# Two places per slot, in place of three, where a projection stream is interrupted, and VectorE and ScalarE steps placed anew

## The chip, the cores and the metric

One core of one Trainium2 chip runs the whole layer. The metric is the device time in microseconds (us) of one execution, as the median of three runs. TensorE is PE in the profile, VectorE DVE, ScalarE ACT, GpSimd POOL, SyncE SP.

## The reference

```python
h = x * (1.0 + scale[:, None, :]) + shift[:, None, :]          # adaLN from c
proj = h @ w_in + b_in                                         # 1024 tokens, 6664 columns
# branch A, 8 heads of 64, per block of 128 queries
z = einsum('bhtd,bhsd->bhts', qb, kb) * scale
log_rem = where(causal, log_sigmoid(-z), 0.0)
suffix = cumsum(log_rem, reverse=True) - log_rem
attn = where(causal, exp(log_sigmoid(z) + suffix), 0.0)        # times v
y_sb = (heads * silu(sb_z)) @ w_sb_proj
# branch B, 4 heads of 128, a gated recurrence computed by chunks
mq, mk = split(silu(causal_depthwise_conv(concat(ml_q, ml_k), conv_w, conv_b)))
hm = head_norm(mlstm_chunkwise(mq, mk, ml_v, i_pre, log_f), ml_norm_g)
y_ml = (hm * sigmoid(ml_o) * silu(ml_z)) @ w_ml_proj
y = (sigmoid(g_sb) * y_sb + sigmoid(g_ml) * y_ml) @ w_out
out = layer_norm(2 ** 0.25 * x + (1 + gate) * y, ln_g, ln_b)
```

## The kernel before

A prologue builds h, transposed, as a high and a low part (hH, hL; the weights likewise, wH, wL), so that each fp32 product is three fp32r matmuls. Then comes a loop of four iterations i = 0 to 3, then the remaining gate projections, the merge of the branches and the output with its norm. The change touches the loop.

One iteration computes one pair of attention heads (branch A), one mLSTM head (branch B), and the projections of the next. The projections are a stream of 432 matmuls of 128x512 (`project(i, lo, hi)`, L617): nine jobs of 48, numbered 0 to 431, each job in two halves that fill proj_ps[0] and [1]. All other PE work interrupts this stream. After the first 48 come twelve slots s = 0 to 11, then a tail of 45. A slot is a block of 128 queries against up to 512 keys; `n_keys(s)` is 128, 256, 384, 512, 128, 512, 256, 512, 384, 512, 512, 512.

What a slot s does, in order of its data: PE makes the scores of both heads h into z_ps[0] and [1] (`scores`, L701 to L703). ACT takes exp into ez (`odds`, L973). DVE caps and masks it (`cap_odds`, L1462, L1465). ACT takes ln(1 + e), then exp of its negative, into rem (`remainders`, L982, L986). DVE scans rem backwards (`stick_left`, L1478, one scan per head). POOL multiplies ez by it (L556): these are the attention weights. In the next slot PE transposes them, 128x128 at a time (`turn_weights`, L716), into at_ps, which is bank 7 for both heads, and ACT copies them to SBUF (`turned`, L994). Then PE multiplies them by v (`weighted_values`, L732).

Because at_ps is one bank, head 1's transposes wait until ACT has copied head 0's out (semaphore at_out), and they are made at different places in the stream:

```python
scores(i, s)
project(i, a, b)
if s > 0:
    turn_weights(i, s - 1, 0)
mlstm_first(i, s)
project(i, b, c_)
if s > 0:
    turn_weights(i, s - 1, 1)
mlstm_second(i, s)
mlstm_third(i, s)
project(i, c_, d)
if s > 0:
    weighted_values(i, s - 1)
```

Branch B uses misc_ps[0] and [1]. `conv_sum(i, k)` on DVE, k = 0 to 3, computes the two halves of the convolution of k (k = 0, 1) and of q (k = 2, 3); `conv_exps`, `conv_bound`, `conv_sigmoid` and `conv_silu` turn it into m_k (index 0) and m_q (index 1). `chunk_weights` and `mask_chunk_weights` make the chunk weights m_w. `mlstm_third` transposes m_k in slot 2 and m_v in slot 3. In slots 4 to 11 a chunk cc = s - 4 goes through PE (`mlstm_first`, L745 to L752), DVE (`chunk_scores`, L1567, L1569), PE (`mlstm_second`, L759) and DVE (`chunk_values`, L1579 to L1587). The first needs m_q, and both misc banks drained by the step that used them last.

Each engine runs its own list in order, so a wait holds up all that stands behind it. The place of an ACT or DVE step among projections is set by `events`: a number of stream position for each evacuation, weight split and gate step (o_log, z_log, z_exp, z_mul); `tasks(i, lo, hi)` issues those of a stretch. Steps of other kinds hang on the slots through `place0`, `place1` and `place2`, which stand behind the first, the second and again the second stretch of a slot.

## Time and profile before

| what | value |
|---|---|
| three runs | 1025.34, 1029.36, 1030.14 us, median 1029.36 us |
| the profiled execution | 1025.17 us, of which its span 1023.4 us |
| PE busy | 953.4 us, 93% of the span |
| DVE busy | 602.2 us, 59% |
| ACT busy | 457.2 us, 45% |
| POOL busy | 173.0 us, 17% |
| mean granted TensorE clock | 0.981 of full speed |

The span runs from the first to the last instruction of one profiled execution. Busy time is the sum of an engine's instructions; matmuls overlap, so PE at 93% does not say how near it is to its peak. In the loop, the transposes of L716 run from 136.0 to 681.1 us of the span.

### The profile page before, as it was taken

Reading aid. Unit: us, or ns where it says so; the run is one execution under the profiler, and the core shown is the slowest. Engines: PE = TensorE matmul, PEld = TensorE weight load, DVE = VectorE, ACT = ScalarE, POOL = GpSimd, SP = SyncE. Lnnn points to the kernel's source line nnn. Section 1 sums busy time; section 2 is a strip of 40 time slices with the busy share of each in tenths; the row PEclk is TensorE's granted clock in tenths of the full one; section 3 lists DMA queues with packets and bytes.
Section 4 is the critical chain, followed back from the end, with each engine's and each line's share of the span. In section 5 each row is a group of like instructions: output and inputs, shape, how many; then the busy total and the mean of one; then the engine's idle time right before and its main releaser. Section 6 shows DMA issues by size and latency. Waiting matters only on the chain.

```text
span 1023.4 us, 14224 instructions
## 1 busy us (share of the span) xinstructions
PE 953.4 (93%) x4965; PEld 754.4 (74%) x4965; DVE 602.2 (59%) x1100; ACT 457.2 (45%) x811; POOL 173.0 (17%) x145
## 2 busy tenths in 40 slices
PE   2399999899999899998999998999999999988995
PEld 1367877677877688776788776788778888866883
DVE  2854786564875566865657856553653333264766
ACT  1133456554475463665554765434743222251221
POOL 1101021322032231122420132311100000001220
PEclk9689999999999999999999999999999999999998
DMA  8702121011311102211113111115712111233232
GB/s 287 250 11 67 43 63 42 22 34 29 93 40 41 31 20 61 72 40 31 30 31 93 42 31 33 31 50 165 242 58 73 50 42 41 93 105 101 83 105 100
DMA packets 78083, 73.64 MB, mean 72 GB/s; under 512 B 4792, under 2 KB 66360, under 8 KB 78044
## 3 DMA queue, kind: packets, MB, share of 16 engines
q1 hardware_dynamic: 73116, 58.31, 19.8%
q0 software_dynamic: 2624, 8.54, 2.5%
q10 hardware_dynamic: 2304, 6.29, 1.6%
q8 instruction: 23, 0.38, 0.2%
q14 instruction: 16, 0.13, 0.0%
HBM read 64.59 MB, written 8.40 MB: 71 GB/s over the span
## 4 chain that ended last, share of the span: by engine, by line
PE 86%; DVE 4%; ACT 4%; issue 3%; DMA 2%; SPq 1%; POOL 0%; ACTq 0%; DVEq 0%; POOLq 0%
PE bank L617 45%; PE bank L597 9%; PE bank L599 9%; PE bank L598 9%; PE bank L732 3%; PE bank L716 3%; PE bank L701 2%; PE bank L686 1%; DMA x_rows<-in_x 1%; ACT rem L982 1%; DMA a_raw<-in_w_ada 1%; PE bank L703 1%; PE bank L702 1%; DVE a_acc L1302 1%; PE bank L759 1%
## 5 line engine op out<-in xcount | busy, mean ns | idle before, releaser
L617 PE MATMUL bank<-hH,wH 128*128 128x512 f32 x704 | 288.7, 410 | 0.6 <-DVE wL L1316 0.6
L617 PE MATMUL bank<-hH,wL 128*128 128x512 f32 x704 | 276.7, 393 | 0.0
L617 PE MATMUL bank<-hL,wH 128*128 128x512 f32 x704 | 275.5, 391 | 0.0
L556 POOL TENSOR_TENSOR ez<-ez,rem 128x512 f32<-128x512 f32 (+3 forms) x96 | 135.0, 1425 | 423.4 <-DVE rem L1478 423.4
L1316 DVE SCALAR_TENSOR_TENSOR wL<-w_raw,wH 128x512 fp32r<-128x512 f32 (+1 forms) x122 | 94.0, 772 | 142.3 <-ACT wH L901 141.2
L617 PEld LDWEIGHTS bank<-hH,wH 128*128 128x128 f32 x704 | 132.5, 188 | 35.7 <-issue 10.6
L617 PEld LDWEIGHTS bank<-hH,wL 128*128 128x128 f32 x704 | 132.2, 188 | 29.3
L617 PEld LDWEIGHTS bank<-hL,wH 128*128 128x128 f32 x704 | 132.7, 189 | 24.6 <-issue 1.0
L901 ACT ACTIVATE wH<-w_raw 128x512 fp32r<-128x512 f32 (+1 forms) x122 | 75.5, 621 | 103.1 <-PE bank L599 76.2
L1478 DVE TENSOR_TENSOR_SCAN rem<-rem,ones 128x512 f32<-128x512 f32 (+3 forms) x96 | 88.5, 964 | 28.5 <-ACT rem L986 28.5
L994 ACT ACTIVATE at<-bank 128x512 f32<-128x512 f32 (+3 forms) x96 | 46.2, 481 | 42.3 <-PE bank L716 42.3
L973 ACT ACTIVATE ez<-bank 128x512 f32<-128x512 f32 (+3 forms) x96 | 41.8, 488 | 50.0 <-PE bank L703 49.5
L716 PE MATMUL bank<-ident,ez 128*128 128x128 f32 x288 | 47.9, 275 | 13.9 <-ACT at L994 13.9
L1462 DVE TENSOR_SCALAR ez<-ez 128x512 f32<-128x512 f32 (+3 forms) x80 | 27.5, 344 | 53.5 <-ACT ez L973 52.5
L716 PEld LDWEIGHTS bank<-ident,ez 128*128 128x128 f32 x288 | 35.7, 139 | 29.8 <-ACT at L994 20.4
L597 PE MATMUL bank<-hH,wH 128*128 128x512 f32 (+1 forms) x144 | 57.4, 399 | 0.0
L598 PE MATMUL bank<-hL,wH 128*128 128x512 f32 (+1 forms) x144 | 57.4, 399 | 0.0
L586 POOL TENSOR_TENSOR yL<-yT,yH 128x1024 fp32r<-128x1024 f32 x6 | 17.2, 2861 | 236.2 <-ACT yH L1243 236.2
L599 PE MATMUL bank<-hH,wL 128*128 128x512 f32 (+1 forms) x144 | 57.1, 396 | 0.0
L597 PE MATMUL bank<-hH,yH 128*128 128x512 f32 x128 | 51.9, 406 | 5.4 <-POOL yL L586 3.0
L599 PE MATMUL bank<-hH,yL 128*128 128x512 f32 x128 | 52.1, 407 | 0.0
L598 PE MATMUL bank<-hL,yH 128*128 128x512 f32 x128 | 52.0, 407 | 0.0
(234 smaller groups left out, 1466.1 us busy)
## 6 DMA issues: line engine op xcount, KB each, us to landing
w_raw<-in_w_in SPq DMA_DIRECT2D x104, 256.0 KB, 2.9
a_raw<-in_w_ada SPq DMA_DIRECT2D x16, 512.0 KB, 4.6
x_rows<-in_x SPq DMA_DIRECT2D x8, 512.0 KB, 7.7
raw<-in_w_ada POOLq DMA_DIRECT2D x8, 512.0 KB, 5.9
x_in<-in_x SPq DMA_DIRECT2D x8, 512.0 KB, 4.0
out_y<-res SPq DMA_DIRECT2D x8, 512.0 KB, 2.9
raw<-in_w_out SPq DMA_DIRECT2D x10, 256.0 KB, 4.3
m_w<-bm_scratch ACTq DMA_DIRECT2D x4, 512.0 KB, 4.0
```

Source lines behind the costliest of these rows:

```text
L556: g.tensor_tensor(e, e, r, ALU.mult).then_inc(a_done[h], 1)
L597: t.matmul(ps, aH, bH, start=k == 0, stop=False)
L598: t.matmul(ps, aH, bL, start=False, stop=False)
L599: return t.matmul(ps, aL, bH, start=False, stop=k == kt - 1)
L617: ins = t.matmul(proj_ps[half][:], w, a, start=(r == 0), stop=(r == JOB_MM // 2 - 1))
L716: ins = t.transpose(at_ps[:, b * P:(b + 1) * P], ez[s % 2][h][:, b * P:(b + 1) * P], ident[:])
L732: ins = t.matmul(y_ps[64 * h:64 * h + 64, tt], v_tok[:, j, 64 * h:64 * h + 64], at_sb[h][:, b * P:(b + 1) * P], start=b == 0 and not conti ...
L901: a.activation(wH[:, slot, :, 0:width], w_raw[:, slot, :, 0:width], ACT.Copy, scale=scale)\
L973: a.activation(ez[s % 2][h][:, 0:w], z_ps[h][:, 0:w], ACT.Exp).then_inc(ex_done[h], 1)
L994: a.activation(at_sb[h][:, 0:w], at_ps[:, 0:w], ACT.Copy).then_inc(at_out[h], 1)
L1316: v.scalar_tensor_tensor(out=wL[:, slot, :, 0:width], in0=w_raw[:, slot, :, 0:width], scalar=scale, in1=wH[:, slot, :, 0:width], op0=ALU.m ...
L1478: v.tensor_tensor_scan(back, back, ones[:, 0:1].to_broadcast((P, w)), first, ALU.mult, ALU.min)\
```

## The change

It does these things:

- `turn_weights` handles both heads in one go and writes into z_ps[0] and [1], from which ACT has taken the exp of this slot's scores by then; bank 7 is not used for it. `scores` of the next slot waits in its turn until ACT has copied the transposed weights out.
- A slot has two interruptions. The first is `mlstm_first`, `weighted_values(s - 2)` and `scores`; the second is both heads' `turn_weights(s - 1)`, `mlstm_second` and `mlstm_third`. Stretches are 8, 8, 16 matmuls in slots 0 to 2, and 7, 6, 14 after (the first two run through on PE); the tail has two stretches in place of three.
- The transposes of next_v move from stream position 24 into slot 0, with ACT's copy.
- On DVE, `chunk_scores` moves ahead of `cap_odds`, and `chunk_values` right behind `stick_left`. `chunk_weights` moves from slot 0 to slot 1, and the mask from slot 1 to slot 2, behind the scans. `conv_bound(1)` stands ahead of the scans of slot 3, `conv_silu(1)` right behind them.
- On ACT, `turned` of both heads stands behind the second stretch's tasks; `conv_exps(1)` and `conv_sigmoid(1)` come earlier in slot 3; the exp of the chunk weights stands behind `conv_sigmoid(0)`.
- The gate steps have separate places for DVE's and ACT's halves (o_cap, z_cap, z_sum are DVE's).

```diff
@@ line 127 @@
...
     at, out = PRE, []
     for s in range(NS):
-        sizes = (10, 10, 12) if s < 3 else (9, 9, 9)
+        sizes = (8, 8, 16) if s < 3 else (7, 6, 14)
         row = [at]
...
@@ line 141 @@
...
     at = segments()[0][-1][-1]
-    third = (JOB_MM * NJ - at) // 3
-    return [at, at + third, at + 2 * third, JOB_MM * NJ]
+    return [at, at + (JOB_MM * NJ - at) // 2, JOB_MM * NJ]
...
@@ line 150 @@
     n = NJ
-    found = [(JOB_MM * 4 + 6, 2, "o_log", 0, 0), (JOB_MM * 5 + 6, 2, "z_log", 0, 0),
-             (JOB_MM * 5 + 14, 2, "z_exp", 0, 0), (JOB_MM * 5 + 22, 2, "z_mul", 0, 0)]
+    found = [(JOB_MM * 4 + 4, 2, "o_cap", 0, 0), (JOB_MM * 4 + 15, 2, "o_log", 0, 0),
+             (JOB_MM * 5 + 4, 2, "z_cap", 0, 0), (JOB_MM * 5 + 20, 2, "z_log", 0, 0),
+             (JOB_MM * 5 + 32, 2, "z_sum", 0, 0), (JOB_MM * 6 + 1, 2, "z_exp", 0, 0),
+             (JOB_MM * 6 + 12, 2, "z_mul", 0, 0)]
     for j in range(n):
...
@@ line 209 @@
...
         proj_ps, z_ps, y_ps, misc_ps = bank[0:2], bank[2:4], bank[4], bank[5:8]
-        at_ps = bank[7]
...
@@ line 693 @@
...
                     r = slice(64 * h, 64 * h + 64)
-                    if s > 0:
+                    if s > 1:
+                        pe.wait_ge(at_out[h], i * NS + s - 1)
+                    elif s > 0:
                         pe.wait_ge(ex_done[h], i * NS + s)
...
@@ line 702 @@
...
-            def turn_weights(i, s, h):
-                if h == 0:
-                    if s > 0:
-                        pe.wait_ge(at_out[1], i * NS + s)
-                    else:
-                        pe.wait_ge(dec_drained, 1)
-                else:
-                    pe.wait_ge(at_out[0], i * NS + s + 1)
-                pe.wait_ge(a_done[h], i * NS + s + 1)
-                for b in range(n_keys(s) // P):
-                    ins = t.transpose(at_ps[:, b * P:(b + 1) * P], ez[s % 2][h][:, b * P:(b + 1) * P], ident[:])
-                ins.then_inc(at_filled[h], 1)
+            def turn_weights(i, s):
+                for h in range(2):
+                    if s + 1 < NS:
+                        pe.wait_ge(ex_done[h], i * NS + s + 2)
+                    pe.wait_ge(a_done[h], i * NS + s + 1)
+                    for b in range(n_keys(s) // P):
+                        ins = t.transpose(z_ps[h][:, b * P:(b + 1) * P], ez[s % 2][h][:, b * P:(b + 1) * P], ident[:])
+                    ins.then_inc(at_filled[h], 1)
...
@@ line 760 @@
...
             def mlstm_third(i, s):
+                if s == 0:
+                    for n in range(2):
+                        pe.wait_ge(m_drained[n], m_count(n, i, F_V))
+                        if n == 0:
+                            pe.wait_ge(drained[1], job(i, -2) + 1)
+                        transposes(n, [next_v[:, cc * P:(cc + 1) * P] for cc in range(4 * n, 4 * n + 4)])
                 if s == 2:
...
@@ line 775 @@
...
                 segs, _ = segments()
-                project(i, 0, 24)
-                for n in range(2):
-                    pe.wait_ge(m_drained[n], m_count(n, i, F_V))
-                    if n == 0:
-                        pe.wait_ge(drained[1], job(i, -2) + 1)
-                    transposes(n, [next_v[:, cc * P:(cc + 1) * P] for cc in range(4 * n, 4 * n + 4)])
-                project(i, 24, PRE)
+                project(i, 0, PRE)
                 for s in range(NS):
-                    a, b, c_, d = segs[s]
+                    start, _, middle, end = segs[s]
+                    mlstm_first(i, s)
+                    if s > 1:
+                        weighted_values(i, s - 2)
                     scores(i, s)
-                    project(i, a, b)
+                    project(i, start, middle)
                     if s > 0:
-                        turn_weights(i, s - 1, 0)
-                    mlstm_first(i, s)
-                    project(i, b, c_)
-                    if s > 0:
-                        turn_weights(i, s - 1, 1)
+                        turn_weights(i, s - 1)
                     mlstm_second(i, s)
                     mlstm_third(i, s)
-                    project(i, c_, d)
-                    if s > 0:
-                        weighted_values(i, s - 1)
+                    project(i, middle, end)
+                weighted_values(i, NS - 2)
                 ends = tail()
                 project(i, ends[0], ends[1])
-                turn_weights(i, NS - 1, 0)
+                turn_weights(i, NS - 1)
                 project(i, ends[1], ends[2])
-                turn_weights(i, NS - 1, 1)
-                project(i, ends[2], ends[3])
                 weighted_values(i, NS - 1)
...
@@ line 991 @@
...
                     act.wait_ge(pv_done[h], i * NS + s)
-                a.activation(at_sb[h][:, 0:w], at_ps[:, 0:w], ACT.Copy).then_inc(at_out[h], 1)
+                a.activation(at_sb[h][:, 0:w], z_ps[h][:, 0:w], ACT.Copy).then_inc(at_out[h], 1)
...
@@ line 1034 @@
...
                         continue
-                    if what == "z_mul":
+                    if what in ("o_cap", "z_cap", "z_sum", "z_mul"):
                         continue
...
@@ line 1095 @@
...
             def place0(i, s):
-                if s == 5:
+                if s == 6:
                     store_y(i, 0)
...
@@ line 1108 @@
...
                     load_forget_row(i)
-                if s == 1:
-                    act.wait_ge(w_sum, i + 1)
-                    a.activation(m_w[:], m_w[:], ACT.Exp).then_inc(w_exp, 1)
-                if s == 3:
-                    conv_exps(i, 1)
+                    token_major(i, F_V, v_tok)
...
                     conv_sigmoid(i, 0)
+                    act.wait_ge(w_sum, i + 1)
+                    a.activation(m_w[:], m_w[:], ACT.Exp).then_inc(w_exp, 1)
                 if s == 3:
                     token_major(i, F_MV, m_vtok)
-                    conv_sigmoid(i, 1)
...
                 tasks(i, -1, 24, last)
-                token_major(i, F_V, v_tok)
                 act.wait_ge(sig_log, i * 2 + 1)
...
                     odds(i, s)
+                    if s == 3:
+                        conv_exps(i, 1)
                     tasks(i, p0, p1, last)
...
                     remainders(i, s)
+                    if s == 3:
+                        conv_sigmoid(i, 1)
+                    tasks(i, p1, p2, last)
                     if s > 0:
                         turned(i, s - 1, 0)
-                    tasks(i, p1, p2, last)
+                        turned(i, s - 1, 1)
                     place1(i, s)
-                    if s > 0:
-                        turned(i, s - 1, 1)
                     place2(i, s)
...
                 turned(i, NS - 1, 0)
-                tasks(i, ends[1], ends[2], last)
                 turned(i, NS - 1, 1)
...
                 a.activation(small[:, 24:32], small[:, 24:32], ACT.Exp, scale=-0.5).then_inc(rstd_exp, 1)
-                tasks(i, ends[2], ends[3], last)
+                tasks(i, ends[1], ends[2], last)
                 store_y(i, 1)
...
@@ line 1489 @@
...
                         continue
-                    if what == "o_log":
+                    if what == "o_cap":
                         for h in range(2):
...
                         v.tensor_scalar(m_gate[:], m_gate[:], EXP_CAP, None, ALU.min).then_inc(o_capped, 1)
-                    elif what == "z_log":
+                    elif what == "z_cap":
                         cap_sig(i * 2 + 1)
-                    elif what == "z_exp":
+                    elif what == "z_sum":
                         dve.wait_ge(sig_log, i * 2 + 2)
...
@@ line 1623 @@
...
             def place0(i, s):
-                if s == 5:
-                    gate_y(i, 0)
                 if s >= 4:
...
@@ line 1633 @@
...
                     conv_bound(i, 0)
-                if s >= 4:
-                    chunk_values(i, s - 4)
...
                     pair_gate(i)
+                if s == 1:
                     chunk_weights(i)
-                if s == 1:
-                    mask_chunk_weights(i)
                     conv_sum(i, 2)
                 if s == 2:
+                    conv_sum(i, 3)
                     weighted_keys(i)
-                    conv_sum(i, 3)
-                if s == 3:
-                    conv_bound(i, 1)
-                    conv_silu(i, 1)
...
@@ line 1660 @@
...
                     p0, p1, p2, p3 = segs[s]
+                    place0(i, s)
                     cap_odds(i, s)
...
                         conv_silu(i, 0)
-                    place0(i, s)
+                    if s == 3:
+                        conv_bound(i, 1)
+                    if s == 5:
+                        gate_y(i, 0)
                     tasks(i, p0, p1, last)
                     stick_left(i, s)
+                    if s == 2:
+                        mask_chunk_weights(i)
+                    if s == 3:
+                        conv_silu(i, 1)
+                    if s >= 4:
+                        chunk_values(i, s - 4)
                     tasks(i, p1, p2, last)
...
```

PE in slot 6, between stretches of L617 (before) and L618 (changed); the rows left out are projections, score terms and further blocks. Before:

```order
L716 MATMUL bank<-ident,ez 128x128 [waits a_done0,at_out1]
L716 MATMUL bank<-ident,ez 128x128
...
L745 MATMUL bank<-m_q,m_k 128x128 [waits misc_drained0]
L750 MATMUL bank<-m_vtok,m_ktok 128x129 [waits misc_drained1]
L752 MATMUL bank<-m_state,m_q 128x129
...
L716 MATMUL bank<-ident,ez 128x128 [waits a_done1,at_out0]
L716 MATMUL bank<-ident,ez 128x128
...
L759 MATMUL bank<-m_vtok,m_s 128x129 [waits misc_drained0]
...
L732 MATMUL bank<-at,v_tok 64x128 [waits at_out0]
L732 MATMUL bank<-at,v_tok 64x128 [waits at_out1]
```

In the changed kernel:

```order
L744 MATMUL bank<-m_q,m_k 128x128 [waits misc_drained0]
L749 MATMUL bank<-m_vtok,m_ktok 128x129 [waits misc_drained1]
L751 MATMUL bank<-m_state,m_q 128x129
L731 MATMUL bank<-at,v_tok 64x128 [waits at_out0]
L731 MATMUL bank<-at,v_tok 64x128 [waits at_out1]
...
L704 MATMUL bank<-kH,qH 128x512 [waits at_out0]
...
L704 MATMUL bank<-kH,qH 128x512 [waits at_out1]
...
L715 MATMUL bank<-ident,ez 128x128 [waits a_done0,ex_done0]
L715 MATMUL bank<-ident,ez 128x128
L715 MATMUL bank<-ident,ez 128x128 [waits a_done1,ex_done1]
L715 MATMUL bank<-ident,ez 128x128
...
L758 MATMUL bank<-m_vtok,m_s 128x129 [waits misc_drained0]
```

The two heads' transposes stand together and wait for the exps (ex_done), the scores wait for the copies (at_out), and mlstm_first stands at the slot's head.

ACT in slot 7 (L973 and L968 exp of scores, L982 to L986 and L977 to L981 remainders, L994 and L989 copies of the turned weights, L1035 the gate's exp, L1026 its ln). Before:

```order
L973 ACTIVATE ez<-bank 128x512 [waits at_filled0,z_done0]
L973 ACTIVATE ez<-bank 128x512 [waits at_filled1,z_done1]
L1035 ACTIVATE sig<-sig 128x1024 [waits z_sum]
...
L982 ACTIVATE rem<-ez 128x512 [waits a_done0,ez_capped0]
L982 ACTIVATE rem<-ez 128x512 [waits a_done1,ez_capped1]
L986 ACTIVATE rem<-rem 128x512 [waits ln_done0]
L986 ACTIVATE rem<-rem 128x512 [waits ln_done1]
L994 ACTIVATE at<-bank 128x256 [waits pv_done0,at_filled0]
...
L923 ACTIVATE next_q<-bank,h_col 128x512 [waits proj_filled0]
L994 ACTIVATE at<-bank 128x256 [waits pv_done1,at_filled1]
```

In the changed kernel:

```order
L968 ACTIVATE ez<-bank 128x512 [waits at_filled0,z_done0]
L968 ACTIVATE ez<-bank 128x512 [waits at_filled1,z_done1]
...
L977 ACTIVATE rem<-ez 128x512 [waits a_done0,ez_capped0]
L977 ACTIVATE rem<-ez 128x512 [waits a_done1,ez_capped1]
L981 ACTIVATE rem<-rem 128x512 [waits ln_done0]
L981 ACTIVATE rem<-rem 128x512 [waits ln_done1]
L1026 ACTIVATE sig<-sig 128x1024 [waits sig_capped]
...
L918 ACTIVATE next_q<-bank,h_col 128x512 [waits proj_filled0]
L989 ACTIVATE at<-bank 128x256 [waits pv_done0,at_filled0]
L989 ACTIVATE at<-bank 128x256 [waits pv_done1,at_filled1]
```

The gate step between the exps and the remainders, which waits for a sum on DVE, has gone to slot 8; another, whose input is capped in the slot before, stands behind the remainders.

DVE from the last step of m_k in slot 2 on (L1541 and L1534 conv_silu(0), L1478 and L1471 scans, L1316 and L1309 weight splits, L1560 and L1553 weighted keys, L1527 to L1531 and L1520 to L1524 conv_sum(3)). Before:

```order
L1541 SCALAR_TENSOR_TENSOR m_k<-m_num,m_k 128x1024 [waits conv_sig]
L1478 SCALAR_TENSOR_TENSOR rem<-rem,ones 128x384 [waits rem_done0]
L1478 SCALAR_TENSOR_TENSOR rem<-rem,ones 128x384 [waits rem_done1]
...
L1316 SCALAR_TENSOR_TENSOR wL<-w_raw,wH 128x512 [waits wH_done]
...
L1560 TENSOR_TENSOR m_ktok<-bank,h_tok 128x512 [waits misc_filled0]
...
L1560 TENSOR_TENSOR m_ktok<-bank,h_tok 128x512 [waits misc_filled1]
L1527 TENSOR_SCALAR m_q<-conv_in,h_col 128x512 [waits proj_drained1]
...
L1531 SCALAR_TENSOR_TENSOR m_q<-conv_in,h_col,m_q 128x512 [waits dve_step]
...
L1316 SCALAR_TENSOR_TENSOR wL<-w_raw,wH 128x512 [waits wH_done]
```

In the changed kernel:

```order
L1534 SCALAR_TENSOR_TENSOR m_k<-m_num,m_k 128x1024 [waits conv_sig]
L1471 SCALAR_TENSOR_TENSOR rem<-rem,ones 128x384 [waits rem_done0]
L1471 SCALAR_TENSOR_TENSOR rem<-rem,ones 128x384 [waits rem_done1]
L1546 TENSOR_TENSOR m_w<-m_w,notbefore 128x1024 [waits w_exp]
L1520 TENSOR_SCALAR m_q<-conv_in,h_col 128x512 [waits proj_drained1]
...
L1524 SCALAR_TENSOR_TENSOR m_q<-conv_in,h_col,m_q 128x512 [waits dve_step]
...
L1553 TENSOR_TENSOR m_ktok<-bank,h_tok 128x512 [waits misc_filled0]
...
L1553 TENSOR_TENSOR m_ktok<-bank,h_tok 128x512 [waits misc_filled1]
...
L1309 SCALAR_TENSOR_TENSOR wL<-w_raw,wH 128x512 [waits wH_done]
...
L1309 SCALAR_TENSOR_TENSOR wL<-w_raw,wH 128x512 [waits wH_done]
```

The mask of the chunk weights (L1546) now follows the scans of slot 2, and conv_sum(3) stands ahead of the weighted keys, which no longer have a split ahead of them.

## Rows read from the trace of the kernel before

**Rows 1.** The page: shares of the chain that ended last, by engine.

```profile
PE 86%; DVE 4%; ACT 4%; issue 3%; DMA 2%; SPq 1%; POOL 0%; ACTq 0%; DVEq 0%; POOLq 0%
```

**Rows 2.** Waits of PE: us in total, times, longest.

```profile
PE bank L716 <- ACT at L994: 13.9, 12, 2.9
```

**Rows 3.** Timeline of PE: start us, us, operation, idle before; iteration 2, slot 7.

```profile
486.76 0.44 PE L716 MATMUL bank<-ident,ez 128*128 128x128 f32 x2 [2.94 <-ACT at L994]
```

**Rows 4.** Timelines of ACT, then DVE, same slot.

```profile
483.30 1.06 ACT L1035 ACTIVATE sig<-sig 128x1024 f32<-128x1024 f32 x1 [3.60 <-DVE sig L1501]
...
482.05 1.22 DVE L1501 TENSOR_TENSOR sig<-sig,m_gate 128x1024 f32<-128x1024 f32 x1
```

**Rows 5.** Timeline of PE, iteration 2, around slot 4.

```profile
447.70 0.39 PE L617 MATMUL bank<-hH,wL 128*128 128x512 f32 x1
448.02 0.88 PE L732 MATMUL bank<-at,v_tok 128*64 128x128 f32 x12
...
449.32 0.50 PE L617 MATMUL bank<-hH,wH 128*128 128x512 f32 x1
...
453.03 0.40 PE L617 MATMUL bank<-hH,wL 128*128 128x512 f32 x1
...
454.42 0.39 PE L617 MATMUL bank<-hH,wL 128*128 128x512 f32 x1
...
455.54 0.39 PE L617 MATMUL bank<-hL,wH 128*128 128x512 f32 x1
```

**Rows 6.** Timeline of DVE, iteration 2, slots 1 to 2.

```profile
420.15 1.23 DVE L1548 TENSOR_TENSOR m_w<-m_w,h_tok 128x1024 f32<-128x1024 f32 x1
...
426.06 0.69 DVE L1316 SCALAR_TENSOR_TENSOR wL<-w_raw,wH 128x512 fp32r<-128x512 f32 x1 [1.21 <-ACT wH L901]
...
427.27 1.22 DVE L1553 TENSOR_TENSOR m_w<-m_w,notbefore 128x1024 f32<-128x1024 f32 x1
428.40 0.54 DVE L1527 TENSOR_SCALAR m_q<-conv_in,h_col 128x512 f32<-128x512 f32 x1
...
431.22 0.29 DVE L1462 TENSOR_SCALAR ez<-ez 128x256 f32<-128x256 f32 x1
...
432.03 1.22 DVE L1541 SCALAR_TENSOR_TENSOR m_k<-m_num,m_k 128x1024 f32<-128x1024 f32 x1
433.69 1.81 DVE L1478 TENSOR_TENSOR_SCAN rem<-rem,ones 128x384 f32<-128x384 f32 x2 [0.44 <-ACT rem L986]
435.44 1.41 DVE L1316 SCALAR_TENSOR_TENSOR wL<-w_raw,wH 128x512 fp32r<-128x512 f32 x1
436.78 1.28 DVE L1560 TENSOR_TENSOR m_ktok<-bank,h_tok 128x512 f32<-128x512 f32 x2
```

**Rows 7.** Timeline of PE, iteration 2: m_k transposes, then mlstm_first of slot 4.

```profile
434.74 1.04 PE L686 MATMUL bank<-ident,m_k 128*128 128x128 f32 x8
...
451.90 0.39 PE L745 MATMUL bank<-m_q,m_k 128*128 128x128 f32 x2
```

**Rows 8.** Groups of DVE by form, loop: same operation behind and clear of scans.

```profile
L1536 DVE TENSOR_SCALAR sig<-sig 128x1024 f32<-128x1024 f32 x4 | 6.9, 1728 | 0.0
...
L1536 DVE TENSOR_SCALAR m_num<-m_num 128x1024 f32<-128x1024 f32 x4 | 2.7, 685 | 0.0
```

**Rows 9.** Timelines of ACT, then DVE, iteration 2, slot 3.

```profile
441.98 1.15 ACT L982 ACTIVATE rem<-ez 128x512 f32<-128x512 f32 x2 [0.85 <-DVE ez L1465]
...
443.69 2.34 DVE L1478 TENSOR_TENSOR_SCAN rem<-rem,ones 128x512 f32<-128x512 f32 x2 [1.27 <-ACT rem L986]
445.94 1.73 DVE L1536 TENSOR_SCALAR sig<-sig 128x1024 f32<-128x1024 f32 x1
```

**Rows 10.** Timelines of PE, then DVE, iteration 2, slot 9.

```profile
500.40 0.51 PE L701 MATMUL bank<-kH,qH 64*128 64x512 f32 x2
...
505.27 2.46 DVE L1478 TENSOR_TENSOR_SCAN rem<-rem,ones 128x512 f32<-128x512 f32 x2 [0.24 <-ACT rem L986]
...
509.29 0.34 DVE L1579 TENSOR_SCALAR m_tmp<-bank,h_tok 128x129 f32<-128x129 f32 x1
```

## The prediction

> **What bounds the kernel now.** I read the page first: PE holds 86% of the chain that ended last [rows 1]. A change to the loop can gain in two ways only: less PE work, or less time in which PE waits. The view of waits gives the second: PE waits for ACT's copy of the turned weights (at, L994) 13.9 us in all, 12 times, so 3 per iteration and 3.5 us of each [rows 2]. It is the one wait of PE inside the loop that is worth an edit. The longest of the three lies in slot 7: 2.94 us before head 1's transposes [rows 3]. Its cause is on ACT and DVE: the gate's exp (L1035) stands ahead of the remainders and waits 3.60 us for a sum (L1501) that DVE starts only at 482.05; everything behind it on ACT, the copy of head 0 too, is late by that much [rows 4].
>
> **The change, term by term.** Times are for one iteration, then times four.
>
> *A. The waits of at.* Head 1's transposes no longer share a bank with head 0's, and the gate's exp no longer stands ahead of the remainders. ACT's copies are now due only at the next slot's `weighted_values`, some 4 us later (14 projections of 0.23 us, and `mlstm_first`). The pitch 0.23 is 1.39 us over six starts, 453.03 to 454.42 [rows 5]. All of 13.9 us goes: -13.9.
>
> *B. One interruption fewer per slot.* From 454.42 to 455.54 is 1.12 us for two projections (0.46) and a block of four transposes and mlstm_second (six instructions, 0.44 of it the transposes) [rows 5]; that is the work itself, and what a block of 128-column transposes costs beyond it I cannot tell from zero. Entering `weighted_values` does cost: 0.32 us after the last projection, at 447.70 to 448.02, where the pitch is 0.23 [rows 5]; that entry stays, behind `mlstm_first`. So B is 0, with bounds of -0.1 and +0.1 per slot (both from this entry), which I take at 0 since full-width blocks enter free. The transposes of next_v move with the same work: 0.
>
> *C. The transposes of m_k in slot 2 need `conv_silu(0)`.* Before, DVE was done with it at 433.2 (432.03 and 1.2) and PE asked at 434.74: 1.5 us in hand [rows 6, 7]. In the changed kernel `chunk_weights` stands where the mask stood, 1.87 us (1.26 from 420.15 on, and a second step of 0.6) for 1.13 (427.27 to 428.40) [rows 6], so DVE is 0.74 us later; and PE comes after 32 projections of the two slots where it came after 36, so 0.9 us earlier. That leaves -0.1: a wait of about 0.2 us, +0.8 in four iterations (bounds 0 and +2).
>
> *D. `mlstm_first` of slot 4 needs `conv_silu(1)` and stands at the slot's head.* This is the largest term against. PE, from the transposes of m_k to that point: 17.2 us before (434.74 to 451.90) [rows 7]; five projections fewer (1.1), no `weighted_values` and no scores of slot 4 (together 1.5: 447.70 to 449.32 less one pitch, and 0.1 at the exit), one block of four transposes fewer (0.4), and a short wait of 0.1 gone [rows 5]: 14.0 us. DVE, from the end of `conv_silu(0)`, which is the same moment: scans of 384, 1.75 (433.69 to 435.44); the mask, 1.13; `conv_sum(3)`, 2.8 as `conv_sum(2)` (428.40 to 431.22); weighted keys, 1.2 (the 1.28 of the pair, less the overlap with the next); two splits, 1.25 (0.69 each, as at 426.06, less the overlap); the cap of head 0 in two steps, 0.5 (a little over the 0.4 of slot 2's, 431.22 on) [rows 6]. That is 8.6. From there ACT's logarithms and exps take 1.75 until the scans start (441.98 to 443.69, and the handover), the scans 2.25 (443.69 to 445.94) [rows 9], `conv_silu(1)` 1.2: 13.8. So far no wait. But one row says that what follows scans is held up. The same operation, 1024 elements, took 1728 ns right behind the scans of slot 3 and 685 ns elsewhere [rows 8], and the split right behind the scans of slot 2 took 1.41 us where clear of scans it takes 0.69 (435.44 and 426.06) [rows 6]. POOL's product of head 0 runs at those times. In the changed kernel the mask stands behind the scans of slot 2 and `conv_silu(1)` behind those of slot 3: +0.7 and +1.0, and some 0.2 for the second product inside `conv_sum(3)`. DVE is then done at 15.8, 1.8 us after PE asks. Bounds: 0.4 without any of it (the sigmoid on ACT and the copy of the last m_v bank come then last) and 2.3 with another full hold. I take 1.8, since both rows lie where the steps will stand: +7.2 (bounds +1.6 and +9.2).
>
> The Trainium skill (SBUF — State Buffer, "Who interferes with whom") has a rule for this: VectorE with two SBUF inputs, or in a two-port mode, and GpSimd lock each other out for a whole instruction. By that rule the three two-input steps of `conv_sum(3)` are candidates too, and D would be nearer 2.3 than 1.8.
>
> *E. The other slot heads.* `mlstm_first` of slots 5 to 11 needs `chunk_values` of the slot before. The tightest is slot 9 of 512 keys with an evacuation ahead: before, from the start of its scores (500.40) to the end of the scans 7.25 us (505.27 and 2.38), and 0.65 for the two steps that drain the banks, each as the 0.34 of m_tmp: 7.9 [rows 10]. PE comes back after scores 0.9, 13 projections 3.0, six transposes 0.7, mlstm_second 0.2 and 14 projections 3.2, with 0.1 for the exit of the block: 8.1. In hand: 0.2 us; in the other 512-key slots, which have no evacuation there or start later on PE, about 0.7 (the 0.6 of an evacuation more). So E is 0 (upper bound 0.3 per iteration, +1.2). Weight splits, gate steps and stores stay hidden: DVE and ACT are idle before the next exps, and if that cover were gone each would cost its own 0.6 to 1.2 us. SP's loads and POOL's products keep their order.
>
> **Sum.** -13.9 + 0.8 + 7.2 + 0 = -5.9 us. Against the profiled execution of 1025.2 us that is 1019.3. That execution and the three runs lie 5 us apart (1025.2 to 1030.1) with a mean of 1027.5, so for a median I forecast **1021.5 us**, 0.8% under the median shown of 1029.36 and 0.6% under that mean.
>
> **Rivals.**
> 1. *All is covered.* The holds don't occur (POOL's product happens to run later), D is 0.4 and C is 0. -13.9 + 1.6 = -12.3: 1015. For it: the sum without holds is 13.8 against 14.0. Against it: both rows of holds. Chance 0.17.
> 2. *The hold spreads.* Each two-input step of DVE behind a scan is held by the product of POOL. D is 2.3, C 0.5, E 0.3, so 3.1 per iteration: -13.9 + 12.4 = -1.5, 1026. For it: 1.04 and 0.72 us in the rows where it could be seen [rows 6, 8]. Against it: most steps behind scans in slots 4 to 11 read PSUM, and slot 9 shows none. The page's rule cited above is this rival's. Chance 0.28.
> 3. *Slower: the slot heads become the bound.* PE now stands still at every `mlstm_first` until DVE has drained the banks of the slot before; before, it came to that point after scores and nine projections, 3 us later. If the chain exp, cap, ln, exp, scan, values is later by L than I have it, slot 9 costs L - 0.2 and three more slots L - 0.7 each. It decides from L = 1.3: 1.1 + 1.8 = 2.9 per iteration, 11.6 in all, a net of +5.7. At L = 1.5 it is 1.3 + 2.4 = 3.7, so +8.9: 1036. For it: a chain of seven handovers with 0.2 us in hand. Against it: the chain's length is measured [rows 10]. Chance 0.13.
> My own case has 0.42.
>
> **Chances and range.** About 0.5%, 5 us, is what a measurement of this kernel can tell from no change. Faster by more: rival 1 (0.17), four fifths of my case (0.34), a little of rival 2: 0.52. Within: a fifth of my case (0.08), and 0.23 of rival 2: 0.31. Slower: rival 3 (0.13) and the rest of rival 2: 0.17. The range runs from 1013, rival 1 with B's gain, to 1032, rival 2 with the upper bounds of C and E and the scatter of the runs. My own case alone is 1017 to 1026.
>
> **What would show each step.** A: the wait of PE's transposes for ACT (at) falls from 13.9 us to under 1. D: in slot 4, PE idle before `mlstm_first` for 1 to 2.3 us, released by DVE's m_q or by the copies of m_v; DVE's `conv_silu(1)` over 2 us long instead of 1.2. C: a wait of some tenths before the transposes of m_k. The mask in slot 2 about 1.9 us long. E: in slots 5 to 11 no wait above 0.3 us. B: the pitch from block to block unchanged. Wrong would be: waits at most slot heads (rival 3), no wait in slot 4 (rival 1), or a wait on scores for the copies, which I have at none since ACT is done 3 us ahead.

## The result, and the profile after

The changed kernel takes **1021.68 us** (median of 11 runs, 1017.64 to 1022.96), the kernel before, run beside it on the same chip, 1027.53 us (11 runs, 1024.6 to 1030.76). The ratio is 0.9934 with a 95% interval of 0.9919 to 0.995: 0.66% faster (the two medians lie 5.85 us, 0.57%, apart). The profiled execution of the changed kernel took 1021.37 us with a span of 1019.6 us and a mean granted clock of 0.975; that of before 1025.17, 1023.4 and 0.981.

The page of the changed kernel: the engines, the clock by slices, and the chain by engine.

```profile
PE 955.2 (94%) x4965; PEld 765.9 (75%) x4965; DVE 600.2 (59%) x1100; ACT 456.5 (45%) x811; POOL 177.3 (17%) x145
...
PEclk9689998999999999999999999999999999999998
...
PE 82%; DVE 10%; issue 2%; ACT 2%; DMA 2%; SPq 1%; POOL 0%; DVEq 0%; ACTq 0%; POOLq 0%
```

DVE's part of the chain went from 4% to 10% and ACT's from 4% to 2% [rows 1]: what PE waits for has changed hands. The view of PE's waits between 120 and 700 us, where the four iterations lie, has one row where it had another one before [rows 2]:

```profile
PE bank L744 <- DVE m_q L1534: 8.4, 4, 2.1
```

So the wait for `at` is gone altogether, and in its place stands one wait per iteration, of the first chunk matmul of slot 4 (`mlstm_first`) for `conv_silu(1)`. PE's timeline of iteration 2 there (columns as in [rows 3]):

```profile
448.20 0.48 PE L744 MATMUL bank<-m_q,m_k 128*128 128x128 f32 x2 [2.12 <-DVE m_q L1534]
...
450.22 0.42 PE L705 MATMUL bank<-kL,qH 64*128 64x128 f32 x2
...
451.81 0.63 PE L618 MATMUL bank<-hH,wL 128*128 128x512 f32 x1
452.24 0.63 PE L618 MATMUL bank<-hH,wH 128*128 128x512 f32 x1
...
454.04 0.39 PE L618 MATMUL bank<-hH,wH 128*128 128x512 f32 x1
454.27 0.40 PE L618 MATMUL bank<-hL,wH 128*128 128x512 f32 x1
```

The wait is the one forecast. What follows it was not: the projections start 0.43 us apart at 452, where at 454 they are back at 0.23. The view by windows says why (columns: window, its length, busy time of PE, PEld, DVE, ACT and POOL, granted clock, DMA share, GB/s), behind the waits of iterations 0 and 2:

```profile
164.00:166.00 2.00, 2.00 (x19) 1.55 (x15) 0.06 (x1) 0.00 (x0) 0.00 (x0) 0.50 0.00 0
166.00:168.00 2.00, 2.00 (x5) 1.61 (x6) 1.10 (x4) 1.35 (x6) 0.10 (x1) 0.50 0.00 0
168.00:170.00 2.00, 2.00 (x6) 1.55 (x6) 0.13 (x1) 0.00 (x0) 0.80 (x2) 0.54 0.00 0
...
450.00:452.00 2.00, 2.00 (x11) 1.69 (x10) 0.50 (x2) 0.92 (x5) 0.00 (x0) 0.50 0.00 0
452.00:454.00 2.00, 2.00 (x8) 1.57 (x7) 0.74 (x2) 0.44 (x3) 0.91 (x2) 0.72 0.00 0
```

The granted clock is at the lower of its two levels (0.5, that is 1.2 GHz) for some 6.8 us in iteration 0 and 3.4 us in iteration 2, and at 1.00 everywhere else in the iterations. The trace of before has no such stretch in its iterations.

What the stretches cost can be read from the lengths of the iterations, taken from the scores of slot 0 to the next scores of slot 0. In the changed kernel:

```profile
123.53 0.34 PE L704 MATMUL bank<-kH,qH 64*128 64x128 f32 x2
...
267.93 0.34 PE L704 MATMUL bank<-kH,qH 64*128 64x128 f32 x2
...
409.25 0.34 PE L704 MATMUL bank<-kH,qH 64*128 64x128 f32 x2
...
552.09 0.34 PE L704 MATMUL bank<-kH,qH 64*128 64x128 f32 x2
```

and before:

```profile
268.72 0.34 PE L701 MATMUL bank<-kH,qH 64*128 64x128 f32 x2
...
412.15 0.34 PE L701 MATMUL bank<-kH,qH 64*128 64x128 f32 x2
```

Before, an iteration lasts 143.4 us. After, iterations 0, 1 and 2 last 144.40, 141.32 and 142.84. Iteration 1, which has no stretch, is 2.1 us shorter than before; beside it the stretch of 6.8 us cost 3.1 and the one of 3.4 us cost 1.5. Four iterations without a stretch would save 8.4 us; less the 4.6 of the two stretches this is 3.8, the difference of the two spans.

DVE in iteration 2, slots 2 to 4, where the terms C and D stand:

```profile
430.62 1.22 DVE L1534 SCALAR_TENSOR_TENSOR m_k<-m_num,m_k 128x1024 f32<-128x1024 f32 x1
431.75 1.80 DVE L1471 TENSOR_TENSOR_SCAN rem<-rem,ones 128x384 f32<-128x384 f32 x2
433.47 1.98 DVE L1546 TENSOR_TENSOR m_w<-m_w,notbefore 128x1024 f32<-128x1024 f32 x1
435.37 1.24 DVE L1520 TENSOR_SCALAR m_q<-conv_in,h_col 128x512 f32<-128x512 f32 x1
...
443.58 2.34 DVE L1471 TENSOR_TENSOR_SCAN rem<-rem,ones 128x512 f32<-128x512 f32 x2 [0.67 <-ACT rem L981]
446.14 1.93 DVE L1534 SCALAR_TENSOR_TENSOR m_q<-sig,m_q 128x1024 f32<-128x1024 f32 x1 [0.22 <-ACT sig L1084]
```

The mask takes 1.98 us where it took 1.22, the first step of `conv_sum(3)` 1.24 where it took 0.54, and `conv_silu(1)` 1.93 where `conv_silu(0)` takes 1.22 [rows 6]. POOL's products lie beside them:

```profile
432.78 3.55 POOL L557 TENSOR_TENSOR ez<-ez,rem 128x384 f32<-128x384 f32 x2 [8.72 <-DVE rem L1471]
444.89 4.31 POOL L557 TENSOR_TENSOR ez<-ez,rem 128x512 f32<-128x512 f32 x2 [8.56 <-DVE rem L1471]
```

### The profile page after: what moved, and what is told of

Its sections match the earlier page's. It is cut to its first block, busy times and chain, and to the rows that moved or that the text cites. A ratio compares the mean times of both kernels' runs of the same rounds, so it can differ in the third digit from the quotient of the medians.

```text
span 1019.6 us, 14219 instructions
## 1 busy us (share of the span) xinstructions
PE 955.2 (94%) x4965; PEld 765.9 (75%) x4965; DVE 600.2 (59%) x1100; ACT 456.5 (45%) x811; POOL 177.3 (17%) x145
## 4 chain that ended last, share of the span: by engine, by line
PE 82%; DVE 10%; issue 2%; ACT 2%; DMA 2%; SPq 1%; POOL 0%; DVEq 0%; ACTq 0%; POOLq 0%
PE bank L618 42%; PE bank L598 9%; PE bank L599 9%; PE bank L600 9%; PE bank L731 3%; PE bank L715 3%; PE bank L704 1%; DVE m_q L1522 1%; DMA x_rows<-in_x 1%; DMA a_raw<-in_w_ada 1%; PE bank L744 1%; DVE a_acc L1295 1%; DVE m_q L1534 1%; DVE m_w L1546 1%; PE bank L687 1%
## 5 line engine op out<-in xcount | busy, mean ns | idle before, releaser
L618 PE MATMUL bank<-hH,wH 128*128 128x512 f32 x704 | 282.3, 401 | 0.7 <-DVE wL L1309 0.7
L618 PE MATMUL bank<-hL,wH 128*128 128x512 f32 x704 | 280.3, 398 | 0.0
L618 PE MATMUL bank<-hH,wL 128*128 128x512 f32 x704 | 276.2, 392 | 0.0
L557 POOL TENSOR_TENSOR ez<-ez,rem 128x512 f32<-128x512 f32 (+3 forms) x96 | 139.2, 1470 | 415.4 <-DVE rem L1471 415.4
L1309 DVE SCALAR_TENSOR_TENSOR wL<-w_raw,wH 128x512 fp32r<-128x512 f32 (+1 forms) x122 | 90.8, 748 | 150.7 <-ACT wH L896 149.9
L618 PEld LDWEIGHTS bank<-hH,wH 128*128 128x128 f32 x704 | 132.9, 189 | 39.9 <-issue 10.7
L618 PEld LDWEIGHTS bank<-hH,wL 128*128 128x128 f32 x704 | 133.1, 189 | 27.6
L618 PEld LDWEIGHTS bank<-hL,wH 128*128 128x128 f32 x704 | 133.1, 189 | 25.4 <-issue 1.0
L1471 DVE TENSOR_TENSOR_SCAN rem<-rem,ones 128x512 f32<-128x512 f32 (+3 forms) x96 | 88.6, 965 | 39.0 <-ACT rem L981 39.0
L968 ACT ACTIVATE ez<-bank 128x512 f32<-128x512 f32 (+3 forms) x96 | 41.9, 489 | 97.2 <-PE bank L706 97.2
L977 ACT ACTIVATE rem<-ez 128x512 f32<-128x512 f32 (+3 forms) x96 | 45.0, 518 | 10.8 <-DVE ez L1458 10.6
L981 ACT ACTIVATE rem<-rem 128x512 f32<-128x512 f32 (+3 forms) x96 | 44.4, 510 | 0.0
L989 ACT ACTIVATE at<-bank 128x512 f32<-128x512 f32 (+3 forms) x96 | 41.3, 483 | 5.5 <-PE bank L715 5.5
```

The source lines that it names most:

```text
L557: g.tensor_tensor(e, e, r, ALU.mult).then_inc(a_done[h], 1)
L618: ins = t.matmul(proj_ps[half][:], w, a, start=(r == 0), stop=(r == JOB_MM // 2 - 1))
L968: a.activation(ez[s % 2][h][:, 0:w], z_ps[h][:, 0:w], ACT.Exp).then_inc(ex_done[h], 1)
L977: a.activation(rem[s % 2][h][:, 0:w], ez[s % 2][h][:, 0:w], ACT.Ln, bias=1.0).then_inc(ln_done[h], 1)
L981: a.activation(r, r, ACT.Exp, scale=-1.0).then_inc(rem_done[h], 1)
L989: a.activation(at_sb[h][:, 0:w], z_ps[h][:, 0:w], ACT.Copy).then_inc(at_out[h], 1)
```

## The experiments

Each was run beside the kernel before on one chip; ratios are to it. "The changed kernel" is the one of the diff above.

**The new wait: where does it come from, and what is it worth?** Three ways to take it away, each an edit to the changed kernel.

*e1: the mask one slot later*, behind `conv_silu(1)`, off the chain that leads to it:

```diff
-                    if s == 2:
-                        mask_chunk_weights(i)
                     if s == 3:
                         conv_silu(i, 1)
+                        mask_chunk_weights(i)
```

> The changed kernel, with the mask of the chunk weights moved from behind the scans of slot 2 to behind conv_silu(1) in slot 3. Theory (DVE's list in slots 2 and 3 is what mlstm_first of slot 4 waits for, and the clock falls to half behind that wait): the mask took 1.98 us there, 0.76 of it held up by POOL; conv_silu(1) ends about 1.5 to 2 us earlier, the wait at mlstm_first of slot 4 falls from 2.1 us to 0.0 to 0.6, the granted clock stays at full speed all through the loop (mean 0.979 to 0.981), and the time falls by 8 us for the four waits and up to 5 us for the two stretches at half clock: 1008 to 1014 us. Rival (ACT's copies of m_v, or conv_sigmoid on ACT, come last anyway): the wait stays above 1.5 us and the time at 1018 to 1022 us. Rival on the clock (it falls for another reason, as the work of slot 4): the stretches at half clock stay, and the time is 1013 to 1016 us.

Measured: 1011.6 us, ratio 0.9859 (0.9833 to 0.9885). PE's wait fell from 8.4 to 3.2 us, 0.8 each (expected 0 to 0.6), and no stretch at a clock of 0.5 was left in the iterations. `conv_silu(1)` was as long as before, 1946 ns: it stands behind its own scans with POOL's product beside it, whatever the mask does. The mask had taken 1.9 us of DVE's list, and the wait fell by 1.3 only: the two-input steps of `conv_sum(3)`, which now lie beside POOL's product, were held in their turn, 2.17 us for a pair that takes 1.54 in the changed kernel:

```profile
429.06 2.17 DVE L1522 SCALAR_TENSOR_TENSOR m_q<-conv_in,h_col,m_q 128x512 f32<-128x512 f32 x2
```

*e2: the first chunk's matmuls behind the scores*, so that PE comes to them later:

```diff
-                    mlstm_first(i, s)
                     if s > 1:
                         weighted_values(i, s - 2)
                     scores(i, s)
+                    mlstm_first(i, s)
```

> The changed kernel, with mlstm_first behind weighted_values and scores in the first interruption of a slot, and nothing else. Theory (D is a matter of where on PE the waiting instruction stands): it comes 1.4 us later in slot 4 (0.9 for weighted_values, 0.5 for the scores), so the wait there falls from 2.1 us to about 0.7, minus 5.6 us in four iterations, and the half-clock stretches become rare: 1011 to 1017 us. In slots 5 to 11 chunk_scores then holds up the cap on DVE by about 0.8 us, which the same shift of mlstm_first covers. Rival (chunk_scores ahead of the cap makes the chain of each slot later, and waits appear at the slot heads or at the turned weights): 1022 to 1032 us.

Measured: 1009.73 us, ratio 0.984 (0.9818 to 0.9863), better than expected. PE's waits between 120 and 700 us:

```profile
PE bank L731 <- ACT at L989: 1.8, 4, 0.5
```

The wait for m_q is gone, though mask and `conv_silu(1)` still take 1978 and 1923 ns: the hold costs nothing once it is covered. (What is left is a wait of `weighted_values` in the same slot for a copy, 0.46 us each.) Again the clock stayed at 1.00 in the iterations.

*e5: POOL's products held back* until DVE has done the steps in dispute (stated in POOL's own loop):

```diff
...
+                if s == 2:
+                    pool.wait_ge(conv_acc, i * 4 + 4)
+                if s == 3:
+                    pool.wait_ge(conv_done, i * 2 + 2)
```

> The changed kernel, with two waits added on POOL: its products of slot 2 start only when conv_sum(3) is done, those of slot 3 only when conv_silu(1) is done. DVE's and PE's lists are unchanged. Theory (POOL's products hold up the DVE steps behind the scans): the mask of slot 2 falls from 1.98 to 1.2 us, the first step of conv_sum(3) from 1.24 to 0.55, conv_silu(1) from 1.93 to 1.2; the wait at mlstm_first of slot 4 falls by 2.1 us to 0.0 to 0.5 (the copies of m_v may come last), and 8 to 13 us go: 1009 to 1015 us; the turned weights of slot 2 may then wait for POOL some tenths. Rival (the long durations have another cause, as the access pattern): the steps keep their 1.9 us, the wait stays at 2.1 us, and the time is 1021 us or more.

Measured: 1009.52 us, ratio 0.9833 (0.9811 to 0.9854). The same stretch of DVE, in the profile of e5:

```profile
429.57 1.20 DVE L1550 TENSOR_TENSOR m_w<-m_w,notbefore 128x1024 f32<-128x1024 f32 x1
430.69 0.55 DVE L1524 TENSOR_SCALAR m_q<-conv_in,h_col 128x512 f32<-128x512 f32 x1
...
434.71 2.11 DVE L1313 SCALAR_TENSOR_TENSOR wL<-w_raw,wH 128x512 fp32r<-128x512 f32 x2
...
441.60 1.23 DVE L1538 SCALAR_TENSOR_TENSOR m_q<-sig,m_q 128x1024 f32<-128x1024 f32 x1 [0.22 <-ACT sig L1088]
```

All three holds are gone (0.78, 0.69 and 0.70 us), and by nothing else than moving POOL's work: that shows the cause. But PE still waited 3.1 us, 0.8 each. The postponed product of slot 2 now holds the two weight splits, 2.11 us for the pair where it was 1.28 in the changed kernel. So 2.2 us of holds went and 0.8 came back, which leaves 1.35, and the wait fell by 1.3 (2.12 to 0.81).

**The old wait: the gate steps or the bank?** The change takes away two suspects at once: the gate steps ahead of the remainders, and one bank for both heads with `weighted_values` right behind.

*e4: the kernel before, with nothing but the gate steps split and placed apart* (three of them 1 to 4 stream positions later than in the change):

```diff
-    found = [(JOB_MM * 4 + 6, 2, "o_log", 0, 0), (JOB_MM * 5 + 6, 2, "z_log", 0, 0),
-             (JOB_MM * 5 + 14, 2, "z_exp", 0, 0), (JOB_MM * 5 + 22, 2, "z_mul", 0, 0)]
+    found = [(JOB_MM * 4 + 4, 2, "o_cap", 0, 0), (JOB_MM * 4 + 18, 2, "o_log", 0, 0),
+             (JOB_MM * 5 + 4, 2, "z_cap", 0, 0), (JOB_MM * 5 + 24, 2, "z_log", 0, 0),
+             (JOB_MM * 5 + 32, 2, "z_sum", 0, 0), (JOB_MM * 6 + 2, 2, "z_exp", 0, 0),
+             (JOB_MM * 6 + 12, 2, "z_mul", 0, 0)]
...
```

> The kernel before, with the gate steps of DVE and ACT given places of their own and nothing else (o_cap, o_log at 198 + 12, z_cap, z_log at 264, z_sum, z_exp at 290, z_mul): bank 7, the three interruptions and all convolution steps stay. Theory (term A is the gate steps ahead of the remainders, not the shared bank): the 13.9 us of PE waits for at fall under 2 us, no new wait at slot 4, 1010 to 1014 us, faster than the changed kernel. Rival (the shared bank needs both: head 1's transposes still wait for head 0's copy): 6 us or more of these waits stay, 1018 to 1024 us.

Measured: 1010.3 us, ratio 0.984 (0.9816 to 0.9863). This part alone, with the bank shared and each head's transposes at a place of their own as before, is 11 us faster than the whole change (10 by the two ratios). Its iterations last 140.04 us, for 143.4 before. In e4's view of waits the row of [rows 2] reads:

```profile
PE bank L718 <- ACT at L996: 1.0, 4, 0.2
```

*e8: the other way about*, the kernel of e2 with the gate steps put back at their old places in the stream:

```diff
-    found = [(JOB_MM * 4 + 4, 2, "o_cap", 0, 0), (JOB_MM * 4 + 15, 2, "o_log", 0, 0),
-             (JOB_MM * 5 + 4, 2, "z_cap", 0, 0), (JOB_MM * 5 + 20, 2, "z_log", 0, 0),
-             (JOB_MM * 5 + 32, 2, "z_sum", 0, 0), (JOB_MM * 6 + 1, 2, "z_exp", 0, 0),
-             (JOB_MM * 6 + 12, 2, "z_mul", 0, 0)]
+    found = [(JOB_MM * 4 + 6, 2, "o_cap", 0, 0), (JOB_MM * 4 + 6, 2, "o_log", 0, 0),
+             (JOB_MM * 5 + 6, 2, "z_cap", 0, 0), (JOB_MM * 5 + 6, 2, "z_log", 0, 0),
+             (JOB_MM * 5 + 14, 2, "z_sum", 0, 0), (JOB_MM * 5 + 14, 2, "z_exp", 0, 0),
+             (JOB_MM * 5 + 22, 2, "z_mul", 0, 0)]
...
```

> The kernel of e2 with the gate steps back at the places in the stream that they had before the change (o_cap and o_log at job 4 + 6, z_cap and z_log at job 5 + 6, z_sum and z_exp at job 5 + 14, z_mul at job 5 + 22), with the weights still turned into the score banks. Theory (the waits of the kernel before came from the gate steps ahead of the remainders on ScalarE, whichever bank the transposes fill): a wait of TensorE for ScalarE comes back in slots 6 to 8, 2 to 4 us in each iteration, 1018 to 1026 us. Rival (the shared bank made those waits, and the score banks alone cure them): as e2, 1009.7 us, with no new wait above 0.3 us.

Measured: 1009.07 us, ratio 0.982 (0.9797 to 0.9843). My theory missed: no wait came back (the only one is e2's, 1.9 us for 1.8). ACT's timeline in e8, iteration 2, slot 7, has the late gate exp ahead of the remainder all the same:

```profile
472.72 1.06 ACT L1030 ACTIVATE sig<-sig 128x1024 f32<-128x1024 f32 x1 [1.98 <-DVE sig L1494]
473.69 1.13 ACT L977 ACTIVATE rem<-ez 128x512 f32<-128x512 f32 x2
...
476.34 0.64 ACT L989 ACTIVATE at<-bank 128x256 f32<-128x256 f32 x2
```

The copies are done at 477.0, and in that timeline PE asks for them at 477.25, in `weighted_values` at the head of slot 8; the transposes of head 1, at 473.5, no longer need the copy of head 0. In the kernel before that copy stood between the two heads' transposes, in the middle of the slot. So with the gate steps back, the rest of the change still covered the delay, with 0.3 us to spare. But e8 is a weaker test than e4. The delay was smaller: ACT waits 1.98 us in e8 and not the 3.60 of [rows 4], since DVE begins the sum 2.8 us after the slot's scores, where before it began 4.4 us after them (`chunk_scores`, ahead of it on DVE, follows the scores more closely). Added to e8's copies, the 1.6 us of difference would put them 1.3 us behind PE's request. So e4 shows that placing the gate steps is enough; that the separate banks alone would be was not shown, and by this estimate they would have left a shorter wait.

**Term B.** *e3: the weights' transposes at two places in each slot again*, on the kernel of e2: head 0's one matmul earlier in the stream, head 1's one later.

```diff
...
-                    project(i, start, middle)
+                    project(i, start, middle - 1)
                     if s > 0:
-                        turn_weights(i, s - 1)
+                        turn_weights(i, s - 1, (0,))
+                    project(i, middle - 1, middle + 1)
+                    if s > 0:
+                        turn_weights(i, s - 1, (1,))
...
```

> The kernel of e2 with one thing altered: in every slot the transposes of head 0 stand one matmul earlier in the stream and those of head 1 one matmul later, so that each slot is interrupted twice for the weights as before the change, not once. Theory (term B is nothing, an interruption costs nothing beside its own matmuls): the median of e2, 1009.7 us, within 2 us. Rival (an interruption costs some 0.1 us each by itself, so that the change gained 4 to 5 us there): 4 x 12 slots x 0.1 = 4.8 us more, 1014.5 us.

Measured: 1010.79 us, ratio 0.983 (0.9806 to 0.9854), against 1009.73 and 0.984 for e2. The wait for `at` is 2.7 us for e2's 1.8, 0.9 of the 1.1 us between the medians; 4.8 us is excluded by the intervals. The iterations tell it more sharply: 140.00 us for e2's 139.78, and the longer wait (0.9 us in four) is all of the difference. Here an interruption costs its own matmuls and nothing beside.

**The half clock.** e1, e2 and e5 are 10 to 12 us faster than the changed kernel, where the view of waits gives them 5 to 7. By the lengths of the iterations the two parts can be told apart for e2: its iterations last 139.78 us, 1.5 less than the one without a stretch in the changed kernel, so 6.2 us in four, and the stretches cost 4.6 more. Is it the place of the wait, ahead of chunk matmuls and scores of 128 columns, or the wait itself?

*e7: the wait put back into e2, but inside full-width matmuls:*

```diff
+                    if s == 3:
+                        project(i, middle, end - 4)
+                        pe.wait_ge(conv_done, i * 2 + 2)
+                        project(i, end - 4, end)
...
```

> The kernel of e2 with a wait for conv_silu(1) put back on TensorE, but four matmuls before the end of slot 3's second stretch, in the middle of full-width matmuls, 0.9 us earlier than the changed kernel waits for it at slot 4's start. The wait should last about 2.1 + 0.9 = 3.0 us, as long as those of slot 7 in the kernel before. Theory A (the half clock follows a wait that stands ahead of the light work of slot 4's start: chunk matmuls of 128 columns and scores): no stretch at a clock of 0.5 in the iterations, since 0.9 us of full-width matmuls come behind the wait, and 1009.7 + 4 x (3.0 + 0.25) = 1022.7 us. Theory B (any wait this long at this place in the iteration does it): stretches at 0.5 in one or more of the four iterations, and 1.5 to 3 us more for each, 1025 to 1034 us.

Measured: 1025.75 us (12 runs), ratio 0.9989 (0.9973 to 1.0006), so theory B. The windows of e7, iterations 1 and 2:

```profile
306.00:310.00 4.00, 2.23 (x22) 1.61 (x22) 1.71 (x1) 2.18 (x5) 2.86 (x2) 1.00 0.00 0
...
449.00:453.00 4.00, 3.15 (x16) 2.31 (x16) 0.80 (x1) 1.26 (x3) 1.93 (x1) 0.61 0.00 0
```

Waits of the same length stand in both; three of the four iterations have a stretch at 0.5 behind theirs, iteration 1 has none. The sum of theory A, four waits of 3.0 and 0.25 us each, forgot that the wait of 0.46 us that e2 has in slot 4 is gone from e7: iteration 1, the one without a stretch, lasts 142.09 us, 2.3 more than e2's, so 9.2 us in four. In the same trace the stretch of 6.8 us made its iteration 3.2 longer and the one of 3.4 us 1.5. In the medians e7 lost 16.0 us: the 6.8 beyond the 9.2 are about what the three stretches of the profiled execution cost, one more of 3.4 us being in iteration 3.

*e9: e6 (below) with a wait in slot 7*, the slot of [rows 3]; *e10: the same wait in each of the slots 5 to 11* (`if s >= 5`):

```diff
...
                         turn_weights(i, s - 1)
+                    if s == 7:
+                        pe.wait_ge(at_out[1], i * NS + s)
                     mlstm_second(i, s)
```

> The kernel of e6 (no wait of TensorE over 0.3 us in the iterations) with one wait put in by hand: in slot 7 of each iteration TensorE waits, behind the weights that it has just turned, until ScalarE has copied those of head 1, some 2 us (ScalarE is at that copy 0.9 to 2.9 us after the last transpose in e6's trace). Sum if only idle time counts: 4 x (2.0 + 0.25) = 9 us more than e6, 1015.8 us, and a mean granted clock of 0.98. Theory (what costs the clock is the wait itself, wherever it stands): a granted clock of 0.5 for some us behind one or more of the four waits in most executions, a mean of 0.97 to 0.977, and 1.5 to 6 us more, 1017 to 1022 us. Rival (it depends on the place, and slot 7 is as immune as in the profiled execution of the kernel before): no such stretch and 1015.8 us.

> As e9, with the wait for the copy of head 1 in each of the slots 5 to 11, 28 waits in the four iterations, by the trace of e6 between 0.8 and 2.1 us long each. If only idle time counts: some 28 x (1.3 + 0.25) = 43 us more than e6, 1050 us, with a clock of 0.98. Theory (the length of a wait decides, as e6's and e5's waits below 1 us left the clock at 1 and waits of 2 to 3 us lowered it in 2 or 3 of 4 iterations): the half clock follows only the longest waits, those of slot 7 above all. Rival (how often TensorE stands still decides, not how long): it falls behind the short ones too, in most slots, and the time is over 1060 us.

Measured for e9: 1021.31 us, ratio 0.9942 (0.9923 to 0.9961), mean clocks 0.975 to 0.977, 14.5 us more than e6, as its theory had it (1017 to 1022). The four waits make 7.5 us. PE's timeline and windows of e9 in iteration 0:

```profile
194.80 0.39 PE L622 MATMUL bank<-hH,wH 128*128 128x512 f32 x1
195.03 0.60 PE L719 MATMUL bank<-ident,ez 128*128 128x128 f32 x4
197.53 0.51 PE L762 MATMUL bank<-m_vtok,m_s 128*128 128x129 f32 x2 [1.90 <-ACT at L998]
...
199.12 0.63 PE L622 MATMUL bank<-hL,wH 128*128 128x512 f32 x1
199.55 0.63 PE L622 MATMUL bank<-hH,wL 128*128 128x512 f32 x1
```

```profile
196.00:198.00 2.00, 0.47 (x3) 0.47 (x4) 1.31 (x2) 1.41 (x4) 1.78 (x1) 0.97 0.00 0
198.00:200.00 2.00, 2.00 (x7) 1.52 (x6) 1.88 (x5) 0.00 (x0) 1.61 (x2) 0.50 0.05 12
200.00:202.00 2.00, 2.00 (x8) 1.58 (x7) 0.70 (x1) 0.00 (x0) 0.00 (x0) 0.68 0.00 0
202.00:204.00 2.00, 2.00 (x19) 1.59 (x17) 1.11 (x3) 0.63 (x1) 0.00 (x0) 1.00 0.00 0
```

So slot 7 is not immune, and before the wait PE had run full-width matmuls at 1.00. Three of e9's four waits have such a stretch. Measured for e10: 1060.29 us, ratio 1.0335 (1.0298 to 1.0373). Its 28 waits make 38.1 us; the view of windows has a stretch at 0.5 behind four of the eight waits of 1.8 to 1.9 us (once in slot 7, three times in slot 8) and behind none of the twenty of 0.7 to 1.5 us. The rival (how often, not how long) expected it in most slots and falls on that count, though its time, over 1060 us, was met: that is 38.1 of idle time, 28 x 0.25 = 7 besides and 6.5 for four such stretches (1.6 each by the lengths of the iterations), 52 of the 53.5 us over e6. The theory had named slot 7 above all, and slot 8 led. That length decides stands as a tally and no more: the longest waits also lie in two slots only, behind other waits.

**A version that beats both.** *e6: e5's two waits of POOL, and the first chunk's matmuls behind the scores in slot 4 only:*

```diff
...
-                    mlstm_first(i, s)
+                    if s != 4:
+                        mlstm_first(i, s)
                     if s > 1:
                         weighted_values(i, s - 2)
                     scores(i, s)
+                    if s == 4:
+                        mlstm_first(i, s)
```

> The changed kernel with two alterations together: POOL holds its products of the stages before slots 2 and 3 back (as in e5), and the first chunk's matmuls of slot 4 alone stand behind the scores (as in e2, but in one slot). It should have neither a wait for conv_silu(1) nor one of weighted_values for a copy in slot 3. Theory: the four waits of 0.8 us that e5 kept go, 3.1 us and some 0.25 us each besides, so 1009.5 - 4 = 1005.5 us. Rival: the remaining idle time was not on the path, and all of these versions end at some 1009.5 us because of something that they share.

Measured: **1006.77 us**, ratio 0.9799 (0.9774 to 0.9823), span 1005.0 us: 2.0% under the kernel before and 15 us under the change; the theory had 1005.5. Its view of PE's waits between 120 and 700 us has no row, its iterations last 139.20 us, and its page begins:

```profile
PE 949.8 (95%) x4965; PEld 762.2 (76%) x4965; DVE 596.2 (59%) x1100; ACT 456.8 (45%) x811; POOL 165.5 (16%) x145
```

PE is busy 5.4 us less than in the changed kernel with the same 4965 matmuls, none of which runs at half the clock in the iterations.

## Why the prediction was right, point by point

The total was right, 1021.5 for 1021.68, and so was every place that it named. Two sizes were off and one cost, the clock, had no term; they cancelled in part, so the closeness of the total is partly luck.

**A (-13.9 us): right in kind, and its size low.** All of the wait went. The text gave two reasons, separate banks and the gate steps; e4 shows that the gate steps are enough, and e8 that the rest of the change covers a delay of 1.98 us without them. The view of waits also understates a standstill: idle time is counted from the end of a matmul, drawn at 0.39 us, while the next one would start after 0.23. Slots with a wait in before bear it out, from scores to scores. Slot 7 in iteration 2, before and after:

```profile
477.62 0.51 PE L701 MATMUL bank<-kH,qH 64*128 64x512 f32 x2
...
490.01 0.45 PE L701 MATMUL bank<-kH,qH 64*128 64x384 f32 x2
```

```profile
479.53 0.51 PE L704 MATMUL bank<-kH,qH 64*128 64x512 f32 x2
...
488.74 0.45 PE L704 MATMUL bank<-kH,qH 64*128 64x384 f32 x2
```

It lasted 12.39 us before and 9.21 after, 3.18 for a wait of 2.94; slot 5 took 9.34 and then 8.73, 0.61 for one of 0.34. With some 0.25 us for each of the twelve, A is about -17.

**B (0): right where it could be tested.** Slots 9 and 10, which had no wait or none of note, last 9.66 and 10.11 us before and 9.66 and 10.07 after; e3 shows the same from the other side.

**C (+0.8): right.** The transposes of m_k start at 431.89, the block ahead of them (0.44 us) at 431.29: 0.16 us of waiting, for a forecast of 0.2. `conv_silu(0)` ends at 431.8 (430.62 and 1.22 above), as the sum had it. No run tried it alone; 0.6 us is below what the medians resolve.

**D (+7.2): right in place and mechanism, low in size.** Per iteration the wait is 2.12 and 0.25, so 2.4 us for a forecast of 1.8, +9.4 in all; the upper bound was +9.2. PE asked 13.9 us after the transposes of m_k, for 14.0 in the text; DVE was done 16.2 us after `conv_silu(0)` (431.84 to 448.07), for 15.8. The step that was mis-sized is "+0.7 and +1.0, and some 0.2": e5 gives 0.78 for the mask, 0.70 for `conv_silu(1)`, and 0.69, not 0.2, inside `conv_sum(3)`. Without holds that leaves 0.2, close to the "So far no wait" of the text. The sign "`conv_silu(1)` over 2 us long" was missed by a little, at 1.93. The rule of the Trainium skill (SBUF — State Buffer, "Who interferes with whom"), that VectorE with two SBUF inputs and GpSimd lock each other out for a whole instruction, is borne out by e5 for the mask and `conv_silu(1)`. By that rule the text would have had D nearer 2.3 than the 1.8 it took, and 2.4 came. But its candidates in `conv_sum(3)` were the three two-input steps; in the changed kernel those were free (0.75 each), and the first step, with one tensor and two columns of scalars, was held. In e1, where they lie beside POOL's product, the two-input steps were held too.

**E (0): right.** No wait in slots 5 to 11; rival 3 did not occur.

**What no term had: the clock.** The two stretches at 0.5 cost 4.6 us by the lengths of the iterations. So for the profiled executions the sum reads -17 + 0.6 + 9.4 + 4.6 = -2.4, for a difference of the spans of -3.8. The terms A, C and D make -7.0, where four iterations without a stretch save 8.4: 1.4 us of gain have no name. Most of them lie in slots 0 to 3, which last some 0.4 us less per iteration than the waits and the moved steps account for. B's lower bound of -0.1 per slot would cover them, but no run isolates them.

The medians add the loss in other executions. The eleven runs of after have mean clocks of 0.975 to 0.979, and the one at 0.979 is the shortest (1017.64). The kernel before seems to have such a loss in many executions: over 38 of them the clock lies between 0.974 and 0.981, the twelve at 0.980 or more average 1025.0 us, the twelve at 0.976 or less 1029.3. No trace of one of the latter was kept, so where their clock fell was not seen; but none of the 34 executions of e1 to e6 and e8, which have no wait of 1.8 us or more in the iterations, is below 0.980. The profiled execution of before, at 0.981, was one without the loss, and I took it for typical; "that execution and the three runs lie 5 us apart" was seen, and its reason was not. If so, the median of before carries some 2.5 us of loss (1027.5 less 1025.0) and that of after some 4.6, and the clock adds 2.1 to the comparison. With it the sum is -17 + 0.6 + 9.4 + 2.1 = -4.9 us. Against the forecast -5.9 the errors are -3.1 (A), -0.2 (C), +2.2 (D) and +2.1 (the clock); that the total came out at the measured -5.9 us owes much to their signs, and to the 1.4 us without a name.

**The rivals.** Rival 1 (all is covered, 1015) fell by the two holds; e2 shows what it is worth when the cover is there, and that 1015 was too high, since the undercount per wait and the clock come on top. Rival 2 (1026) had the wait of 2.3 us right; its 0.5 for C and 0.3 for E did not come (0.16 and none), and A was larger than it had it. Rival 3 asked for waits at most slot heads, and there was one.

## What to carry to other kernels

A step that PE needs is best asked for behind other PE work, not at the head of a block: moving each chunk's small matmuls behind the scores was worth 12 us of the 1021 (6.2 by the lengths of the iterations and 4.6 through the clock), while the held operations on VectorE stayed as slow as they were. Before a step is placed on VectorE behind a scan, look at what the scan releases on GpSimd: in this kernel the product starts at that moment and holds a step with two inputs in SBUF, by 0.6 to 0.8 us. And when a wait of TensorE of about 2 us is priced (the stretches here followed waits of 1.8 us and more), compare the mean granted clock of several executions, not of the profiled one alone, as the wait may cost more than itself.

## What the runs showed of the hardware that was not expected

- Behind waits of 1.8 to 3.0 us, in kernels where TensorE is otherwise busy, the granted clock fell to 0.5 for 3.4 or 6.8 us in part of the cases, at a cost of 1.5 to 1.6 or 3.1 to 3.2 us: in the profiled executions 0 of 4 (before), 2 of 4 (after), 3 of 4 (e7), 3 of 4 (e9), 4 of 8 (e10). Behind waits of 0.7 to 1.5 us (e1, e5, e10: 28 of them in theirs) it never did. What decides between waits of equal length stays open. Neither the place in the slot nor the width of the matmuls around it decides alone: the four waits of e7 stand at one place, within the same matmuls, and one of them has no stretch behind it.
- The first step of `conv_sum(3)`, a TENSOR_SCALAR of 128x512 that reads one tensor and takes 0.55 us alone, took 1.24 us beside GpSimd's product. Which of its operands makes it wait was not tried.
- GpSimd's pair of products of slot 3, 512 columns, took 4.31 us in the changed kernel, beside the second scan and `conv_silu(1)`, and 2.50 in e5, held back behind both: the hold goes both ways.
